# Expert u and v rows in one table, one gather per pick into a ring of ten pairs

## What is computed

```
def peer_ffn(h, w_query, sub_keys, u_tab, v_tab):
    ...
        q = (hb @ w_query).reshape(PEER_TOKEN_BLOCK, PEER_HEADS, 2, half)
        s = jnp.einsum("thpd,hpnd->thpn", q, sub_keys).astype(jnp.float32)
        s_top, i_top = lax.top_k(s, PEER_TOPK)
        ...
        best, pos = lax.top_k(cand, PEER_TOPK)
        expert = jnp.take_along_axis(cand_idx, pos, axis=-1)
        gate = jax.nn.softmax(best, axis=-1)
        u = jnp.take(u_tab, expert, axis=0)
        act = jax.nn.gelu(jnp.einsum("thkd,td->thk", u, hb).astype(jnp.float32), approximate=False)
        w = (gate * act).astype(hb.dtype)
        return jnp.einsum("thk,thkd->td", w, jnp.take(v_tab, expert, axis=0))
```

## Time and profile before

| | |
|---|---|
| time, median of 3 runs (lowest to highest) | 3135.87 us (3134.6 to 3137.12) |
| span of the profiled execution | 3143.0 us |
| busy PE, DVE, ACT, POOL | 2695.4, 1879.8, 973.9, 1153.8 us |
| share of the span of the gathers' DMA queue, of 16 engines | 47.6% |
| expert gathers | 1024 of 512 KB |
| moved by DMA | 821.81 MB |

### The profile page before, as it was taken

The page is one execution under the profiler, slowest core; times in us unless marked ns, Lnnn a source line. Parts: engine busy times, 40 slices in busy tenths (PEclk is TensorE's granted clock), DMA queues, the critical chain, the costliest instruction groups (busy, mean ns, idle before and its releaser), DMA issues.

```text
span 3143.0 us, 33811 instructions
## 1 busy us (share of the span) xinstructions
PE 2695.4 (86%) x10890; PEld 1730.8 (55%) x10890; DVE 1879.8 (60%) x4237; ACT 973.9 (31%) x2097; POOL 1153.8 (37%) x1112
## 2 busy tenths in 40 slices
PE   7978788887777797778887777899999999999998
PEld 3524643333333386433333323798748989974698
DVE  1856566666565485865666664665256666634565
ACT  2245222221221222222221211444135454422444
POOL 0400277777777500677777777000000000000000
PEclk9989899988989898899989888899989999999999
DMA  9930599999999932899999999554315545532454
GB/s 302 382 127 1 217 376 394 395 396 384 386 386 387 369 106 75 348 385 389 394 402 398 372 380 399 205 184 156 134 67 168 185 159 185 186 122 83 141 184 151
DMA packets 223785, 821.81 MB, mean 261 GB/s; under 512 B 24880, under 2 KB 25008, under 8 KB 222768
## 3 DMA queue, kind: packets, MB, share of 16 engines
q0 software_dynamic: 159120, 579.41, 47.6%
q1 hardware_dynamic: 62784, 228.17, 21.4%
q10 hardware_dynamic: 1760, 12.70, 1.2%
HBM read 819.13 MB, written 1.05 MB: 261 GB/s over the span
## 4 chain that ended last, share of the span: by engine, by line
PE 56%; POOL 13%; DVE 12%; DMA 11%; issue 6%; ACT 2%; ACTq 0%; SPq 0%; DVEq 0%
PE ps L1652 11%; PE ps L1346 10%; PE ps L1601 8%; POOL arena L784 7%; DMA arena<-experts_v,arena 7%; POOL arena L792 6%; PE ps L1590 6%; PE ps L1592 5%; PE ps L1591 5%; DMA arena<-experts_u,arena 3%; DVE arena L2276 2%; PE ps L1800 2%; PE ps L1871 2%; DMA weights<-stream 2%; PE ps L1352 1%
## 5 line engine op out<-in xcount | busy, mean ns | idle before, releaser
L1652 PE MATMUL ps<-arena 128*128 128x512 f32 x2016 | 1004.5, 655 | 317.8 <-DMA arena<-experts_v,arena 209.9
L1652 PEld LDWEIGHTS ps<-arena 128*128 128x128 f32 x2016 | 410.4, 209 | 904.3 <-issue 769.2
L2197 DVE SCALAR_TENSOR_TENSOR arena<-arena 128x1024 f32<-128x1024 f32 x512 | 622.8, 1226 | 464.5 <-DMA arena<-experts_u,arena 457.5
L784 POOL DMA_INDIRECT arena<-experts_u,arena x512 | 543.7, 1062 | 529.5 <-DVE arena L2181 374.2
L792 POOL DMA_INDIRECT arena<-experts_v,arena x512 | 553.1, 1080 | 156.0 <-issue 124.3
L1969 DVE TENSOR_TENSOR w_lo<-weights,w_hi 128x512 fp32r<-128x512 f32 x528 | 364.4, 691 | 285.2 <-ACT w_hi L872 284.7
L872 ACT ACTIVATE w_hi<-weights 128x512 fp32r<-128x512 f32 x528 | 333.0, 632 | 385.0 <-PE ps L1592 285.4
L1590 PE MATMUL ps<-a_hi,w_hi 128*128 128x256 f32 x1408 | 400.6, 285 | 3.1 <-DVE a_lo L1982 1.6
L1591 PE MATMUL ps<-a_lo,w_hi 128*128 128x256 f32 x1408 | 399.2, 284 | 0.0
L1592 PE MATMUL ps<-a_hi,w_lo 128*128 128x256 f32 x1408 | 399.2, 284 | 0.0
L1346 PE MATMUL ps<-sq,weights 128*128 128x256 f32 (+1 forms) x1472 | 333.5, 387 | 18.6 <-ACT sq L866 9.7
(11 more groups left out here) (258 smaller groups left out, 2553.0 us busy)
## 6 DMA issues: line engine op xcount, KB each, us to landing
weights<-stream SPq DMA_DIRECT2D x433, 512.0 KB, 3.4
arena<-mod_rows_in POOLq DMA_DIRECT2D x71, 512.0 KB, 9.3
arena<-experts_u,arena POOLq DMA_INDIRECT x512, 6.6
arena<-experts_v,arena POOLq DMA_INDIRECT x512, 6.6
mod_rows<-mod_rows_in POOLq DMA_DIRECT2D x9, 512.0 KB, 9.1
arena<-gain_rows ACTq DMA_DIRECT2D x1, 3072.0 KB, 11.5
arena<-rpb_windows ACTq DMA_DIRECT2D x4, 512.0 KB, 15.9
arena<-keys_in ACTq DMA_DIRECT2D x2, 1024.0 KB, 6.2
```

The lines of the kernel that those rows point to most:

```text
L784: pool.indirect_dma_start(out=u_ring[:, k % U_RING, :], out_offset=None, in_=experts_u[l], in_offset=bass.IndirectOffsetOnAxis(ap=expert[: ...
L1652: ins = pe.matmul(ps[:, 2 * b + half, :], diag[:, k % DIAGS, :], v_ring[:, k % V_RING, HALF * half:HALF * (half + 1)], start=(k == TOPK * ...
L2197: dve.scalar_tensor_tensor(out=u, in0=u, scalar=1.0, in1=h_rows[:, b, :], op0=ALU.mult, op1=ALU.mult, accum_out=act_raw[:, k:k + 1]).then_ ...
```

## The change

The two tables of a layer are joined on the host into one, `experts[l]`, with rows of 2048 numbers: u, then v. One indirect DMA per pick fetches both, 128 rows of 8 KB, into a ring of ten pairs, which takes the room of the two rings. POOL no longer waits for `dot_done`; it waits until `v_used` tells that the pair ten back is used. The last four picks have a gelu, a `weigh` and an addition each. The taps' diagonals and late rows lie at the same places under the new buffer's name.

```diff
+PAIR_RING = 10
...
             def peer(l):
                 base = PICKS * l
-                for n in range(GROUPS + 1):
-                    if n < GROUPS:
-                        if n % SPAN == 0:
-                            pool.wait_ge(expert_ready, CHOICES * l + n // SPAN + 1)
-                        for k in range(SPAN * n, SPAN * (n + 1)):
-                            if base + k >= U_RING:
-                                pool.wait_ge(dot_done, base + k - U_RING + 1)
...
-                    if n:
-                        for k in range(SPAN * (n - 1), SPAN * n):
-                            if base + k >= V_RING:
-                                pool.wait_ge(v_used, base + k - V_RING + 1)
...
+                for k in range(PICKS):
+                    if k % TOPK == 0:
+                        pool.wait_ge(expert_ready, CHOICES * l + k // TOPK + 1)
+                    if base + k >= PAIR_RING:
+                        pool.wait_ge(v_used, base + k - PAIR_RING + 1)
+                    pool.indirect_dma_start(
+                        out=pair_ring[:, k % PAIR_RING, :], out_offset=None, in_=experts[l],
+                        in_offset=bass.IndirectOffsetOnAxis(ap=expert[:, k:k + 1], axis=0)) \
+                        .then_inc(pair_landed[k % PAIR_RING], 16)
...
+                def add_row(k):
+                    row, w = v_part[:, k % PAIR_RING, :], act_w[:, k:k + 1]
+                    dve.wait_ge(weighed, WEIGHED * l + GROUPS + k - TURNED)
...
-                weigh(GROUPS - 1)
-                if l == 0:
-                    ada_rows(2)
-                dve.wait_ge(weighed, GROUPS * (l + 1))
+                dots(GROUPS - 1, TURNED, TURNED + 1)
+                weigh(GROUPS - 2)
                 for k in range(TURNED, PICKS):
...
+                    if k + 1 < PICKS:
+                        dots(GROUPS - 1, k + 1, k + 2)
+                    weigh(GROUPS - 1 + k - TURNED)
+                    add_row(k)
+                    if k == TURNED and l == 0:
+                        ada_rows(2)
```

More of the change, by code:

```diff
@@ L358, in bass_two_blocks @@
 def bass_two_blocks(nc, stream, mod_rows_in, c_rows, x_cols, ctx_cols, cols_in, const_in, tab_attn, tab_mix, rpb_windows, keys_in, gain_rows,
-                    experts_u, experts_v, out):
+                    experts, out):
     plan, PL = make_plan()
@@ L485, in bass_two_blocks @@
         padded = V["pad"].rearrange("p (c t) -> p c t", c=KC)
-        tap_diags = [R[name][:, P * k:P * (k + 1)] for name, n in (("keys", EARLY_TAPS), ("u", U_RING * KC)) for k in range(n)]
+        tap_diags = [R[name][:, P * k:P * (k + 1)] for name, n in (("keys", EARLY_TAPS), ("uv", TAP_ROWS * KC)) for k in range(n)]
         assert len(tap_diags) >= TAPS * len(TAPPED)
@@ L525, in bass_two_blocks @@
         late_rows = [V["rows"][:, D * k:D * (k + 1)] for k in range(3)] + \
-            [v_ring[:, k, :] for k in range(LATE_ROWS - 3)]
+            [R["uv"][:, D * (TAP_ROWS + k):D * (TAP_ROWS + k + 1)] for k in range(LATE_ROWS - 3)]
         mod_at = [(l, m) for l, first, end in ADA_PARTS[1:] for m in range(4 * first, 4 * end)]
@@ L587, in bass_two_blocks @@
         expert_ready = sem("expert_ready")
-        u_landed = [sem(f"u_landed{r}") for r in range(U_RING)]
-        v_landed = [sem(f"v_landed{r}") for r in range(V_RING)]
+        pair_landed = [sem(f"pair_landed{r}") for r in range(PAIR_RING)]
         dot_done = sem("dot_done")
@@ L656, in taken, with landed @@
             ins.then_inc(bank_taken[pr.bank], 1)
-        def landed(l, pick_no, ring):
-            before = l * len(range(pick_no % ring, PICKS, ring))
-            return 16 * (before + pick_no // ring + 1)
+        def landed(l, pick_no):
+            before = l * len(range(pick_no % PAIR_RING, PICKS, PAIR_RING))
+            return 16 * (before + pick_no // PAIR_RING + 1)
         NORMS = {"lat": 0, "ctx": 1, "peer0": 2, "conv": 3, "peer1": 4}
@@ L1060, in gate_exps, with gelu @@
                     act.activation(part, part, ACT.Exp).then_inc(gate_exp, 1)
[L1062 to L1065, removed]
+                def gelu(first, end):
+                    act.wait_ge(dot_done, base + end)
+                    act.activation(act_out[:, first:end], act_raw[:, first:end], ACT.Gelu).then_inc(gelu_done, 1)
                 def diagonals(n):
-                    act.wait_ge(weighed, GROUPS * l + n + 1)
+                    act.wait_ge(weighed, WEIGHED * l + n + 1)
                     for k in range(SPAN * n, SPAN * (n + 1)):
@@ L1086, in peer @@
                 gate_exps(1)
-                for n in range(GROUPS + 1):
-                    if 0 < n < GROUPS:
+                for n in range(GROUPS):
+                    if n < GROUPS - 1:
+                        if n:
+                            diagonals(n - 1)
+                        gelu(SPAN * n, SPAN * (n + 1))
+                    else:
                         diagonals(n - 1)
-                    if n < GROUPS:
-                        gelu(n)
+                        for k in range(TURNED, PICKS):
+                            gelu(k, k + 1)
                     if l == 0 and GROUPS - EARLY_TAPS <= n < GROUPS:
@@ L2207, in peer @@
                 wait_taken(dve, pl["rows"][3])
-                for n in range(GROUPS):
+                for n in range(GROUPS - 1):
                     dots(n, SPAN * n, SPAN * n + 1)
@@ L2231, in peer @@
                     dve.tensor_tensor(y_rows[:, 2 + half, :], ps[:, 2 + half, :],
[L2232 removed]
+                                      v_part[:, (PICKS - 1) % PAIR_RING, HALF * half:HALF * (half + 1)], ALU.add) \
                         .then_inc(y_copied, 1)
@@ L2770 @@
     args = [a for name, a in given.items() if not name.startswith("experts")]
-    args += [[given[f"experts_{e}{l}"] for l in range(LAYERS)] for e in "uv"]
+    args += [[given[f"experts{l}"] for l in range(LAYERS)]]
     out = nc.dram_tensor("out", (P, TB, D), F32, kind="ExternalOutput").ap()
```

49 lines of the change are left out of this document (19 added, 30 removed).

## The result

| | before | after |
|---|---|---|
| time, median (lowest to highest), 4 runs each | 3136.49 us (3134.6 to 3143.6) | 3194.56 us (3190.42 to 3197.93) |
| ratio, 95% interval | | 1.0186 (1.0162 to 1.021) |
| span of the profiled execution | 3143.0 us | 3188.3 us |
| POOL busy | 1153.8 us | 615.2 us |
| packets of the gathers' queue | 159120 | 85392 |

The time lies 44.6 us above my 3150 and above the range's end. Two later comparisons gave 1.0192 (1.0159 to 1.0225) and 1.0187 (1.0146 to 1.0227). In three of the six comparisons the kernel before took 3305 to 3327 us instead of 3136, for a cause that stays open (one chip showed both), while the one kernel with joint rows that ran beside both took 3079.3, 3081.4 and 3080.1. So ratios are taken only within a comparison; where two kernels with joint rows are set against each other across comparisons, that rests on this one kernel.

The account below looks back on a forecast made before the run. The DMA engines' transfer of expert rows was taken to bound the two expert stages. Transfer -43, ring stalls +52 and stage ends +5 gave +14 us on the profiled span, 3157, or 3150 us as median; range 3104 to 3186.

Parts of the forecast that it names:

- The slower of the two is the DMA, by 0.03 us: Expert stages before: DMA engines need 1.28 us per 4 KB-row gather, POOL 1.25 per issue, so DMA sets the pace.
- slow spells: Stretches of low DMA rate in the expert stages, such as 333 GB/s; 0.15 us per pick on average, in clumps.
- my check of a stage: One expert stage before: 655 us of transfer, 13 of query tiles, 4.5 first landing, against 711; 38 us left over.
- Part 1: Expert gathers: one of 8 KB rows per pick at 424 GB/s, 2.473 us against 2.557; -43 us.
- Part 2: POOL's queue: 512 issues fewer, 640 us of POOL time, covered by the DMA and so worth nothing.
- Part 3: Ring of ten pairs: late release behind 28 chooses costs 3.3 us each, 0.7 in ten with query tiles; +52 us.
- Part 4: End of each expert stage: 5.5 us from last landing to PE's start in place of 3.0; +5 us for both layers.
- B: Expert stages: fewer scattered reads shrink the periods of low DMA rate, saving up to 38 us; 3126 to 3136, chance 0.12.
- A: Ring of pairs: it never starves the DMA, so only faster transfer and longer end remain; 3098 us, chance 0.18.
- C: Expert gathers: 8 KB rows are no faster than 4 KB ones; 3183 us, or 3200 if POOL needs longer; chance 0.13.
- D: Behind each choose: a drained DMA queue refills in 6.6 rather than 4.5 us; from about 3165 up, chance 0.10.

Follow-up runs that it names:

- the one kernel with joint rows: The change, ring still ten pairs, with each choose-group's weigh, diagonals and values put ahead of the choose; 3080.12 us, ratio 0.9827 to the kernel before.
- Version 5: The change with each choose-group's weigh, diagonals and values ahead of the choose, and a ring of eleven pairs; 3054.54 us, ratio 0.9751 to the kernel before.

## Why the prediction was wrong, step by step

The sign and the ring's mechanism were right. The size of its stalls was off, and the premise on what paces the kernel before was false. The two errors have opposite signs: the gain was 44 us larger than I had it, the stalls 87 us. That the time is only 44.6 us off is in part luck.

- **"The slower of the two is the DMA, by 0.03 us"**: false, and the root of what parts 1 and 2 have wrong. 0.95 was the median of a distribution with a tail to 1.98; by the mean POOL needs 1.375 per gather against 1.28. The chain of the page of before even names POOL with 13% of the span. My argument that POOL "never waited long for a released buffer" proves the opposite of what I took from it: an engine that never waits is the one that paces. The 38 us of "slow spells" in my check of a stage were POOL's late supply.
- **Part 1, transfer, -43**: the rate was nearly right (421 GB/s, not 424; by it 512 x 0.067 = -34). But with POOL no longer the bound, the gain is from POOL's 1408 us to the DMA's 512 x 2.49 + 26 for the query tiles = 1301: up to 107. Version 5 (experiment 5), in which the ring hardly stalls, took 81.5 us less than the kernel before with the tail's +5 in it: **-87**. The estimate of -15 by the Trainium skill (DMA: Bandwidth & Descriptors, section "Why small descriptors are slow (HBM only)") was farther off than the windows: the gathers' own rates, 410 and 421, differ by 2.7%, not by 1.1%.
- **Part 2, POOL, "worth nothing"**: mis-sized at 0. It has the 53 us of the 87 that the faster transfer (34) doesn't explain; that is a remainder and not a measurement of its own.
- **Part 3, stalls, +52**: 3194 - 3054.5 = **139.5 us**, 5.0 per `choose`; 4.9 by the run without chooses. This is the term that failed most. The windows around the chooses give the same without a comparison of times: 151 us lost, 10 in version 5. The 18 chooses without query products lose 6.6 each where I had 3.3. Of the missing part, 1.97 is PE's first pick and the release at the lower clock (4.06 for 2.09); the rest, about 1.4, is further pairs that arrive late, the next dots waiting 1.57, 1.34 and 1.67. The ten with query tiles lose 3.2 where I had 0.7. That they lose less was right: the four of them at a granted clock of 0.50 to 0.64 lose 4.1, 2.5 less than the 18, which is what two query tiles take (2.6), and the six at 1.00 lose 2.5. What I took off for slow spells was wrong, as the spells were POOL's, and with joint rows POOL has time to spare.
- **Part 4, end, +5**: right. After the change:

```profile
1097.10 1.23 DVE L2190 SCALAR_TENSOR_TENSOR arena<-arena 128x1024 f32<-128x1024 f32 x1
...
1099.95 1.29 DVE L2205 SCALAR_TENSOR_TENSOR arena<-arena 128x1024 f32<-128x1024 f32 x1
...
1102.62 2.28 PE L1405 MATMUL ps<-con,sq 128*128 128x128 f32 x16 [2.61 <-DVE sq L2231]
```

  From the last pair's dot to PE's start 5.5 us, forecast 5.5; from its landing at 1096.8, 5.8, where there had been 3.0.
- **Sum**: -87 + 139.5 + 5 = +57.5, measured +58. This closes by construction, since -87 and 139.5 are both taken from version 5's time; what stands apart from it are the 151 - 10 = 141 us of the windows, and the 5.8 and 3.0 us of the end.
- **Rivals**: B, the spells shrink, was true, for a reason that I had not named (POOL's long gathers, not the reads themselves), and hidden under the larger stalls. A was wrong as the change stands, but it is what version 5 makes true. C fell: 421 GB/s, and 54% of the packets. D, "a stall of over 5 us per `choose`", is what came, though not by a slow refill (5.57 as forecast) but by the late release.

## What to carry to other kernels

Price a repeated instruction by its mean, and check that the price times the count fills the stretch; an engine that fills it without ever waiting is the bound, whatever the DMA share says. When two buffers with short lives become one with a long life, follow the chain from landing to release through every queue that it passes: here a 9 us block stood in it, and moving one group's weights and matmuls ahead of it turned +1.9% into -1.7%, with an eleventh pair -2.5%. A stall in a ring comes back at every turn; other transfers that fall into it cover it only as long as they last (6.6 us without query tiles, 4.1 with two of them at about the same clock).

## What the hardware showed unexpectedly

- Gathers of 8 KB rows ran at 421 GB/s undisturbed, 4 KB rows at 408 to 411; POOL's issue took the same, 0.94 us for the median gather of 128 rows.
- A gather started during DVE's dot ended 0.82 us behind the dot, up to 2.0 us in all.
- With 1 to 1.5 gathers of 4 KB rows open the DMA engines moved 304 to 315 GB/s, with 3 to 4 open 403 to 405, and the share hardly told them apart: it is 0.95 in the window of 333 GB/s.
- After 9.85 us of idle, PE's first pick and the release behind it took 4.06 us at granted clock 0.50, against 2.26 with PE at work before.
